# Second layer's feed-forward up: one piece of 512 columns, with shift times root in its sources

## The chip, the cores and the metric

The kernel runs on one core of one Trainium2 chip. The metric is device time in microseconds (us) of one launch; before the change the median of three runs is 2778.01 us. The core has five engines that run side by side and wait for one another by semaphores: TensorE (PE) for matmuls, VectorE (DVE), ScalarE (ACT), GpSimd (POOL) and SyncE (SP), which here only starts DMAs. PE takes its operands from SBUF and writes to PSUM, in banks of 512 float32 columns.

## The reference

Two layers of a first block, then a second block that the change does not touch. The part that matters is the feed-forward of a layer, for the main stream of 512 tokens with D = 1024 features (in layer 1 also for a context of 256 tokens; in layer 2 the context is no longer needed, `need_ctx` is false):

```python
def rmsnorm(t, g):
    return t * rsqrt(mean(t * t, axis=-1) + EPS) * g
def modulate(t, shift, scale):
    return t * (1 + scale) + shift
def conv_ffn(h, w_up, conv_w, conv_b, w_down):        # w_up: 1024 x 5632
    u = h @ w_up
    up = jnp.pad(u, ((0, 0), (1, 1), (0, 0)))
    u = up[:, :-2] * conv_w[0] + up[:, 1:-1] * conv_w[1] + up[:, 2:] * conv_w[2] + conv_b
    a, b = jnp.split(u, 2, axis=-1)
    return (jax.nn.silu(a) * b) @ w_down
h = h + mx[5] * conv_ffn(modulate(rmsnorm(h, norm2_g[l]), mx[3], mx[4]), w_up[l], ...)
```

## The kernel before

Features lie on the 128 partitions, tokens in the columns, so the residual h is 8 tiles (KT = 8) of 128 partitions x 512 tokens in layer 2. Products are computed to nearly float32 accuracy from rounded operands: a value is split into a high half (rounded, made by ACT) and a low half (the rest, made by DVE), and a product is three matmuls, high x low, high x high and low x high. Each matmul is preceded by one weight load of 128 x 128.

**The stage.** `ffn_up` is one stage: all engines meet at a barrier at its start and end. It has FT = 22 blocks i, each with two halves c (c = 0 goes through Silu, c = 1 is its factor), and for each half (i, c) PE goes through the 8 source tiles k with three products each. The halves' sums lie in two pairs of PSUM areas, by i modulo 2. The high parts of the weights have one room for each c, shared by all blocks: ACT (`high`, L2017) may write the one of (i + 1, c) only when (i, c) is done, and DVE (`low`, L2052) makes the low part after it. The weights come in strips by DMA, one for each block; those of block 0 are split in the stage before.

**The normalisation is deferred.** With g the gain (norm weight times 1 + scale) and s the shift, the product of w with (g x h x r + s) is r x (w, g x h) + (w, s), where r is one over the root of the mean square, a number for each token. So the sources of the matmuls are the tiles g x h, and two columns behind them hold s (for the two streams): 514 columns in layer 2, cut into 256 and 258. They are split by `Deferred.high` and `Deferred.low`, six of eight tiles (LOWS_AHEAD = 6) completely beside the output projection, the stage ahead of this one, through its hooks `add` (on ACT, when DVE has finished a unit of h) and `after` (on DVE). So block 0 can start at once. The squares, their sum, the mean (a matmul with ones, `mean`), Sqrt (`root`) and the reciprocal (`invert`) are made beside blocks 0 and 1.

**What follows a half.** DVE (`evict`): copies the two columns (w, s) out of PSUM to `bias` (L2057), and multiplies the product by r (L2059). ACT (`shift`, L2022) adds the bias. DVE (`convolve`, L2068 to L2070) waits for that and does the convolution over tokens. ACT does Silu (L2027), DVE the product of the halves (L2077). The order on DVE is: low weights of the next block's half, `evict`, `convolve` of the half before, and the product of the block before.

The output projection (`output_projection`, `project`) has 8 units of 512 columns, 8 tiles with three matmuls (L953) each; DVE's sum into h is L1919. After the feed-forward up comes the feed-forward down, again by `project`.

## Time and profile before

| | us |
|---|---|
| median of three runs | 2778.01 |
| the three runs | 2770.65, 2778.01, 2778.29 |
| the profiled execution | 2779.62 |
| its span, first to last instruction | 2777.8 |
| feed-forward up of layer 2, first matmul to last | 1460.1 to 1718.5 |

The profile is of one execution. Times in it count from the start of the span. A matmul's own duration holds the filling and draining of the array, and one starts before the last has ended; the distance between starts is what counts. PEclk is TensorE's granted clock as a share of 2.4 GHz. In a timeline row "xN" says how many instructions in a row it takes together, and the bracket how long the engine stood idle before it and who released it.

### The profile page before, as it was taken

Reading aid. Unit: us, or ns where it says so; the run is one execution under the profiler, and the core shown is the slowest. Engines: PE = TensorE matmul, PEld = TensorE weight load, DVE = VectorE, ACT = ScalarE, POOL = GpSimd, SP = SyncE. Lnnn points to the kernel's source line nnn. Section 1 sums busy time; section 2 is a strip of 40 time slices with the busy share of each in tenths; the row PEclk is TensorE's granted clock in tenths of the full one; section 3 lists DMA queues with packets and bytes.
Section 4 is the critical chain, followed back from the end, with each engine's and each line's share of the span. In section 5 each row is a group of like instructions: output and inputs, shape, how many; then the busy total and the mean of one; then the engine's idle time right before and its main releaser. Section 6 shows DMA issues by size and latency. Waiting matters only on the chain. (4 is left out here: it accounts for less than half of the span.)

```text
span 2777.8 us, 34833 instructions
## 1 busy us (share of the span) xinstructions
PE 2487.8 (90%) x14602; PEld 1933.5 (70%) x14602; DVE 1375.2 (50%) x2185; ACT 868.5 (31%) x1385; POOL 251.7 (9%) x183
## 2 busy tenths in 40 slices
PE   7997988999998998997889999998977889898976
PEld 5885657888887787995669998764733368573322
DVE  4324554566667214325647777347565645423213
ACT  3222433332324113223444334233424642311001
POOL 0002520000000000003500000000042020011112
PEclk9998989999999999997989999999988999988999
DMA  5114731111111112115612223320201013348997
GB/s 240 61 54 106 269 128 46 46 61 61 63 69 38 53 63 82 61 69 142 224 46 92 92 92 117 111 82 31 87 0 54 0 61 137 121 188 326 421 421 292
DMA packets 58555, 326.88 MB, mean 118 GB/s; under 512 B 8157, under 2 KB 14429, under 8 KB 26461
## 3 DMA queue, kind: packets, MB, share of 16 engines
q1 hardware_dynamic: 45358, 302.76, 29.4%
q0 software_dynamic: 5696, 12.59, 1.2%
q10 hardware_dynamic: 7344, 9.28, 1.0%
q8 instruction: 117, 1.92, 0.3%
q14 instruction: 40, 0.33, 0.0%
HBM read 317.26 MB, written 12.58 MB: 119 GB/s over the span
## 5 line engine op out<-in xcount | busy, mean ns | idle before, releaser
L953 PE MATMUL ps<-work_rounded,ring_rounded 128*128 128x512 f32 (+1 forms) x2016 | 537.0, 354 | 19.1 <-DVE work_rounded L397 10.6
L953 PE MATMUL ps<-xn_rounded,ring_rounded 128*128 128x512 f32 (+2 forms) x2304 | 541.8, 347 | 0.0
L2003 PE MATMUL ps<-xn_rounded,ring_rounded 128*128 128x258 f32 (+2 forms) x2816 | 535.1, 312 | 0.0
L2003 PEld LDWEIGHTS ps<-xn_rounded,ring_rounded 128*128 128x128 f32 x2816 | 414.6, 191 | 31.2
L953 PEld LDWEIGHTS ps<-xn_rounded,ring_rounded 128*128 128x128 f32 x2304 | 373.4, 191 | 57.6 <-issue 0.2
L953 PEld LDWEIGHTS ps<-work_rounded,ring_rounded 128*128 128x128 f32 x2016 | 336.5, 192 | 76.3 <-DVE work_rounded L397 11.8
L953 PE MATMUL ps<-big_rounded,ring_rounded 128*128 128x512 f32 (+1 forms) x1200 | 326.3, 364 | 45.0 <-DVE big_rounded L859 25.0
L859 DVE TENSOR_TENSOR ring_rounded<-ring,ring_rounded 128x2048 fp32r<-128x2048 f32 (+2 forms) x94 | 189.1, 2015 | 266.5 <-ACT ring_rounded L824 266.5
L2003 PE MATMUL ps<-work_rounded,ring_rounded 128*128 128x256 f32 (+1 forms) x1232 | 280.2, 309 | 9.0 <-PEq L784 4.8
L953 PEld LDWEIGHTS ps<-big_rounded,ring_rounded 128*128 128x128 f32 x1200 | 203.4, 196 | 84.8 <-DVE ring_rounded L859 21.4
L824 ACT ACTIVATE ring_rounded<-ring 128x2048 fp32r<-128x2048 f32 (+2 forms) x94 | 158.2, 1687 | 314.7 <-PE ps L953 298.3
L2003 PEld LDWEIGHTS ps<-work_rounded,ring_rounded 128*128 128x128 f32 x1232 | 191.9, 191 | 21.5 <-issue 10.6
L2052 DVE TENSOR_TENSOR ring_rounded<-ring,ring_rounded 128x1024 fp32r<-128x1024 f32 x84 | 103.0, 1226 | 171.4 <-ACT ring_rounded L2017 171.4
L2017 ACT ACTIVATE ring_rounded<-ring 128x1024 fp32r<-128x1024 f32 x84 | 89.0, 1060 | 205.8 <-PE ps L2003 205.8
L2022 ACT ACTIVATE work<-work,small 128x512 f32<-128x512 f32 (+1 forms) x132 | 81.5, 649 | 203.0 <-DVE work L2059 203.0
L1313 ACT ACTIVATE big<-big,small 128x512 f32<-128x512 f32 (+1 forms) x81 | 47.0, 624 | 254.0 <-DVE big L1309 154.0
L1303 DVE COPY small<-ps 128x2 f32<-128x2 f32 x46 | 7.3, 159 | 176.9 <-PE ps L953 176.6
L3320 PE MATMUL ps<-big,work 128*64 128x512 f32 x352 | 80.4, 604 | 15.1 <-DMA big<-in_experts 13.8
L1339 POOL MEMSET work<- 128x792 f32 x2 | 1.5, 758 | 1015.4 <-DMA work<-in_pool 1015.4
L2070 DVE SCALAR_TENSOR_TENSOR work<-work,vec 128x769 f32<-128x769 f32 (+1 forms) x88 | 78.0, 887 | 3.1
L2069 DVE SCALAR_TENSOR_TENSOR work<-work,vec 128x769 f32<-128x769 f32 (+1 forms) x88 | 78.0, 887 | 3.1
L3343 ACT ACTIVATE work<-ps,small 128x256 f32<-128x256 f32 x16 | 7.6, 476 | 221.3 <-PE ps L3320 221.3
(420 smaller groups left out, 3125.4 us busy)
## 6 DMA issues: line engine op xcount, KB each, us to landing
ring<-in_stream SPq DMA_DIRECT2D x141, 1024.0 KB, 4.8
big<-in_experts SPq DMA_DIRECT2D x44, 1024.0 KB, 26.0
ring<-in_stream SPq DMA_DIRECT2D x32, 704.0 KB, 4.0
ring<-in_experts SPq DMA_DIRECT2D x22, 1024.0 KB, 27.3
xn<-in_experts SPq DMA_DIRECT2D x15, 1024.0 KB, 28.4
work<-in_experts SPq DMA_DIRECT2D x15, 1024.0 KB, 28.7
big<-in_first_modulation SPq DMA_DIRECT2D x8, 1024.0 KB, 14.1
work<-in_bias ACTq DMA_DIRECT2D x24, 256.0 KB, 3.9
```

The lines of the kernel that those rows point to most:

```text
L824: return act.activation(self.rounded(high), value, ACT.Copy)
L859: return dve.tensor_tensor(self.rounded(value), value, self.rounded(high).bitcast(F32), ALU.subtract)
L953: mm = pe.matmul(out[:, a - u.first:b - u.first], lhs, rhs, start=j == 0 and n == 0 and not u.onto, stop=j == terms - 1 and n == len(passe ...
L1313: act.activation(px[:, m, a:z], px[:, m, a:z], ACT.Identity, bias=bias[:, m, s:s + 1])
L2003: mm = pe.matmul(out[:, a:b], ws[:, k, :], x[k][:, a - base:b - base], start=k == 0 and n == 0, stop=k == KT - 1 and n == 2)
L2017: act.activation(high_w[c], half(i, c)[0], ACT.Copy).then_inc(strip_high.up(), 1)
L2022: ins = act.activation(u[:, i % 2, c, o:o + b - a], u[:, i % 2, c, o:o + b - a], ACT.Identity, bias=bias[:, i % 2, c, s:s + 1])
L2052: dve.tensor_tensor(low_part, value, high_w[c].bitcast(F32), ALU.subtract).then_inc(strip_low.up(), 1)
L2069: settle(dve, dve.scalar_tensor_tensor(out=cc, in0=uu[:, 0:n], scalar=cw(0, t), in1=cc, op0=ALU.mult, op1=ALU.add), vstep)
L2070: dve.scalar_tensor_tensor(out=cc, in0=uu[:, 2:2 + n], scalar=cw(2, t), in1=cc, op0=ALU.mult, op1=ALU.add).then_inc(convolved.up(), 1)
L3320: mm = pe.matmul(b.bank(2)[r, :], self.rows_t[:, k, r], self.gu[s][:, k, :], start=k == 0, stop=k == KT - 1)
L3343: act.activation(self.silu_t, b.bank(2)[:, 0:256], ACT.Silu, scale=b.slot_scale[:, 0, n:n + 1]).then_inc(self.silued, 1)
```

## The change

For layer 2 alone (`need_ctx` false) a class `Rooted` takes the place of `Deferred`. Since g x h x r + s = r x (g x h + s x root), the sources become g x h + s x root, and the product need only be multiplied by r. The two extra columns, their copy and ACT's shift are gone, and a source is 512 columns, one matmul in place of two. In the output projection ACT now writes g x h and the square of each tile, and DVE adds the squares up; the stage begins with the mean and the root, then each tile is shifted by DVE, split by ACT and DVE, and used by both halves of block 0 in turn, tile by tile. Layer 1 computes as before.

The core of the diff ("..." marks what is left out):

```diff
+class Rooted(Deferred):
+    def square(self, act, k):
+        squared, added = self.b.sig("squared"), self.b.sig("squares_added")
+        act.activation(self.rooms[k][0], self.b.x[:, k, :], ACT.Identity, scale=self.gain(k))
+        if k >= 4:
+            act.wait_ge(added.sem, added.at(k - 3))
+        act.activation(self.squares[0] if k == 0 else self.squares[1 + (k - 1) % 3], self.b.x[:, k, :], ACT.Square).then_inc(squared.up(), 1)
+    def add_square(self, dve, k):
...
+    def mean(self, pe, area):
+        pe.matmul(area[:, 0:S], self.b.ones, self.squares[0], start=True, stop=True).then_inc(self.b.sig("summed").up(), 1)
...
+    def shifted(self, dve, k):
+        value = self.rooms[k][0]
+        return dve.scalar_tensor_tensor(out=value, in0=self.root_area, scalar=self.shift(k), in1=value, op0=ALU.mult, op1=ALU.add)
...
-        if next_sources:
+        if type(next_sources) is Rooted:
+            add, after = next_sources.square, next_sources.add_square
+        elif next_sources:
...
-        cuts = [(base, 512), (512, T + 2)]
+        cuts = [(0, 512), (512, T + 2)] if need_ctx else [(0, S)]
...
+                if not need_ctx:
+                    deferred.mean(pe, products[1][1])
+                    for k in range(KT):
+                        pe.wait_ge(tile_low.sem, tile_low.at(k + 1))
+                        for c in range(2):
+                            products_of(0, c, k)
+                    self.strips_freed(1)
...
+                else:
+                    deferred.root(act, products[1][1])
+                    for k in range(KT):
+                        act.wait_ge(tile_value.sem, tile_value.at(k + 1))
+                        deferred.high(act, k).then_inc(tile_high.up(), 1)
+                    high(1, 0)
...
-                    shift(i, c)
+                    if need_ctx:
+                        shift(i, c)
...
-                dve.tensor_copy(bias[:, i % 2, c, :], ps[:, T:T + 2])
+                    if need_ctx:
+                        dve.tensor_copy(bias[:, i % 2, c, :], ps[:, T:T + 2])
...
-                    dve.wait_ge(shifted.sem, shifted.at(2 * i + c + 1))
+                    ready = shifted if need_ctx else evicted
+                    dve.wait_ge(ready.sem, ready.at(2 * i + c + 1))
...
+                else:
+                    dve.wait_ge(self.sig("rooted").sem, self.sig("rooted").at(1))
+                    deferred.shifted(dve, 0).then_inc(tile_value.up(), 1)
+                    for k in range(KT):
+                        if k + 1 < KT:
+                            deferred.shifted(dve, k + 1).then_inc(tile_value.up(), 1)
+                        dve.wait_ge(tile_high.sem, tile_high.at(k + 1))
+                        deferred.low(dve, k).then_inc(tile_low.up(), 1)
                 low(1, 0)
                 deferred.invert(dve)
```

What stands in a row on TensorE at the stage's start, before (L953 ends the output projection, L2003 are the products):

```order
L953 MATMUL ps<-work_rounded,ring_rounded 128x512 x2
L784 UNCONDITIONAL_BRANCH
L1986 UNCONDITIONAL_BRANCH [waits barrier_Pool_Activation_PE_DVE_SP_release]
L2003 MATMUL ps<-work_rounded,ring_rounded 128x256
L2003 MATMUL ps<-work_rounded,ring_rounded 128x258
L2003 MATMUL ps<-xn_rounded,ring_rounded 128x256
L2003 MATMUL ps<-xn_rounded,ring_rounded 128x258
```

and after (L477 is the mean, L2045 are the products):

```order
L1000 MATMUL ps<-work_rounded,ring_rounded 128x512 x2
L831 UNCONDITIONAL_BRANCH
L2039 UNCONDITIONAL_BRANCH [waits barrier_Pool_Activation_PE_DVE_SP_release]
L477 MATMUL ps<-work,base 128x512
L2045 MATMUL ps<-work_rounded,ring_rounded 128x512 [waits tile_low]
L2045 MATMUL ps<-xn_rounded,ring_rounded 128x512 x2
L2045 MATMUL ps<-work_rounded,ring_rounded 128x512
L2045 MATMUL ps<-xn_rounded,ring_rounded 128x512 x2
L2045 MATMUL ps<-work_rounded,ring_rounded 128x512 [waits tile_low]
```

The mean has moved from the front of block 1 to the front of block 0, every sixth matmul of block 0 waits for a tile's low half, and a pair has become one.

On VectorE, from the last sum of the output projection to the first scaling, before (L394 and L397 are the last two low halves, L412 adds squares, L448 is the reciprocal):

```order
L1919 SCALAR_TENSOR_TENSOR h<-ps,mods,h 128x512 [waits product_done]
L784 UNCONDITIONAL_BRANCH
L2047 UNCONDITIONAL_BRANCH [waits barrier_Pool_Activation_PE_DVE_SP_release]
L394 SCALAR_TENSOR_TENSOR work_rounded<-h,gains,xn_rounded 128x512
L397 TENSOR_TENSOR work_rounded<-mods,xn_rounded 128x2
L394 SCALAR_TENSOR_TENSOR work_rounded<-h,gains,xn_rounded 128x512
L397 TENSOR_TENSOR work_rounded<-mods,xn_rounded 128x2
L412 TENSOR_TENSOR work<-work 128x512 [waits squared]
L412 TENSOR_TENSOR work<-work 128x512 [waits squared,squares_added] x6
L2052 TENSOR_TENSOR ring_rounded<-ring,ring_rounded 128x8x128 [waits strip_high,squares_added]
L448 RECIPROCAL big<-big 128x512 [waits rooted]
```

and after, the start (L474 adds squares, L486 shifts a tile, L906 is its low half):

```order
L474 TENSOR_TENSOR work<-work 128x512 [waits squared]
L831 UNCONDITIONAL_BRANCH [waits squares_added]
L2119 UNCONDITIONAL_BRANCH [waits barrier_Pool_Activation_PE_DVE_SP_release]
L486 SCALAR_TENSOR_TENSOR work<-big,mods,work 128x512 [waits rooted]
L486 SCALAR_TENSOR_TENSOR work<-big,mods,work 128x512
L906 TENSOR_TENSOR work_rounded<-work,xn_rounded 128x512 [waits tile_high]
L486 SCALAR_TENSOR_TENSOR work<-big,mods,work 128x512
```

and, eight tiles on, its end (L2124 are low halves of weights, L495 the reciprocal, L2132 the scaling):

```order
L906 TENSOR_TENSOR work_rounded<-work,xn_rounded 128x512 [waits tile_high] x2
L2124 TENSOR_TENSOR ring_rounded<-ring,ring_rounded 128x8x128 [waits strip_high]
L495 RECIPROCAL big<-big 128x512
L2132 TENSOR_TENSOR work<-ps,big 128x512 [waits product_done,zeroed,vector_step]
L2124 TENSOR_TENSOR ring_rounded<-ring,ring_rounded 128x8x128 [waits strip_high]
```

The first DVE instructions of the stage now wait for the root, and the last adding of squares has moved ahead of the barrier; the reciprocal stays between the low weights of (1, 0) and those of (1, 1).

## Rows read from the trace of the kernel before

**Rows 1.** The page, first part: each engine's busy time and share.

```profile
PE 2487.8 (90%) x14602; PEld 1933.5 (70%) x14602; DVE 1375.2 (50%) x2185; ACT 868.5 (31%) x1385; POOL 251.7 (9%) x183
```

**Rows 2.** TensorE's waits in the stage, with releaser: total, times, longest us.

```profile
PE ps L2003 <- DVE ring_rounded L2052: 2.2, 1, 2.2
PE ps L2003 <- PEq L784: 2.0, 1, 2.0
```

**Rows 3.** Table by stretches: output projection, then the stage, both at full clock.

```profile
core 0: us, PE busy (x) PEld busy (x) DVE busy (x) ACT busy (x) POOL busy (x), PEclk, DMA share, GB/s
1417.27:1457.70 40.43, 40.43 (x176) 32.83 (x175) 16.77 (x24) 11.23 (x18) 0.00 (x0) 1.00 0.22 78
1482.13:1718.54 236.41, 236.40 (x1968) 236.20 (x1968) 180.71 (x280) 90.97 (x114) 0.00 (x0) 1.00 0.24 87
```

**Rows 4.** The same table for the first layer's feed-forward up.

```profile
540.00:850.00 310.00, 310.00 (x1759) 271.94 (x1758) 196.59 (x294) 94.09 (x129) 0.00 (x0) 1.00 0.18 64
```

**Rows 5.** Timeline where the stage starts: start us, length us, engine, line, operation.

```profile
1458.14 0.75 DVE L1919 SCALAR_TENSOR_TENSOR h<-ps,mods,h 128x512 f32<-128x512 f32 x1 [3.81 <-PE ps L953]
1458.93 0.72 ACT L387 ACTIVATE xn_rounded<-h,gains 128x512 fp32r<-128x512 f32 x1 [4.48 <-DVE h L1919]
1459.55 0.19 ACT L389 ACTIVATE xn_rounded<-mods 128x2 fp32r<-128x2 f32 x1
...
1460.08 5.03 ACT L405 ACTIVATE work<-h 128x512 f32<-128x512 f32 x8 [0.33 <-PEq L784]
```

**Rows 6.** Timeline: a mean's matmul at full clock; 768 columns at half.

```profile
1473.19 1.02 PE L437 MATMUL ps<-work,base 128*128 128x512 f32 x2
...
1109.81 2.93 PE L437 MATMUL ps<-work,base 128*128 128x512 f32 x4 [2.77 <-DVE work L412]
```

**Rows 7.** Timeline of ScalarE: Sqrt, and a table load with what follows it.

```profile
1474.25 0.60 ACT L443 ACTIVATE big<-ps 128x512 f32<-128x512 f32 x1 [4.19 <-PE ps L437]
...
1487.27 1.28 ACT L2027 ACT_TABLE_LOAD   x1
1488.56 0.63 ACT L2027 ACTIVATE work<-work 128x512 f32<-128x512 f32 x1
```

**Rows 8.** VectorE: splits in the output projection; a group, its count, total, mean ns.

```profile
1410.00 4.91 DVE L859 TENSOR_TENSOR big_rounded<-big,work_rounded 128x512 fp32r<-128x512 f32 x8 [1.02 <-ACT work_rounded L824]
...
1428.30 2.29 DVE L859 TENSOR_TENSOR ring_rounded<-ring,ring_rounded 128x2048 fp32r<-128x2048 f32 x1 [1.96 <-ACT ring_rounded L824]
...
L412 DVE TENSOR_TENSOR work<-work 128x512 f32<-128x512 f32 x7 | 4.8, 691 | 0.2
```

**Rows 9.** Table by stretches where stages start; PEclk 0.50 is 1.2 GHz.

```profile
1457.70:1461.15 3.45, 1.45 (x11) 1.08 (x10) 1.80 (x4) 1.89 (x5) 1.09 (x1) 0.99 0.55 188
1461.15:1464.56 3.41, 3.41 (x19) 3.41 (x18) 3.27 (x7) 3.09 (x7) 1.59 (x1) 0.51 0.30 123
1411.34:1416.46 5.12, 5.12 (x14) 3.97 (x12) 4.59 (x7) 4.07 (x6) 0.00 (x0) 0.50 0.00 0
1724.58:1730.90 6.32, 6.32 (x15) 4.97 (x16) 5.69 (x10) 6.32 (x13) 0.00 (x0) 0.51 0.82 247
```

**Rows 10.** ScalarE's weight splits (a group); VectorE's and TensorE's rows before half (1, 1).

```profile
L2017 ACT ACTIVATE ring_rounded<-ring 128x1024 fp32r<-128x1024 f32 x42 | 44.5, 1059 | 63.6 <-PE ps L2003 63.6
...
1474.88 3.35 DVE L448 RECIPROCAL big<-big 128x512 f32<-128x512 f32 x1 [4.80 <-ACT big L443]
...
1480.76 1.23 DVE L2052 TENSOR_TENSOR ring_rounded<-ring,ring_rounded 128x1024 fp32r<-128x1024 f32 x1 [1.74 <-ACT ring_rounded L2017]
...
1482.13 0.47 PE L2003 MATMUL ps<-work_rounded,ring_rounded 128*128 128x256 f32 x2 [2.17 <-DVE ring_rounded L2052]
```

**Rows 11.** Timeline where the stage's matmuls have ended.

```profile
1718.57 0.16 DVE L2057 COPY small<-ps 128x2 f32<-128x2 f32 x1 [0.63 <-PE ps L2003]
...
1719.37 0.72 ACT L2022 ACTIVATE work<-work,small 128x512 f32<-128x512 f32 x1 [3.23 <-DVE work L2059]
...
1720.61 0.75 DVE L2070 SCALAR_TENSOR_TENSOR work<-work,vec 128x512 f32<-128x512 f32 x1
```

More of the change, by code:

```diff
@@ L448, in invert, with __init__, root, high @@
         settle(dve, dve.reciprocal(self.rstd, self.rstd), vstep)
+class Rooted(Deferred):
+    def __init__(self, b, l, rooms, squares, root, rstd):
+        self.b, self.rooms, self.root_area, self.rstd = b, rooms, root, rstd
+        self.first, self.width = CTX, S
+        self.squares = tiles_in(S, squares)[0:4]
+        self.gain = lambda k: b.gains[:, l, 0, 1, k:k + 1]
+        self.shift = lambda k: b.mods[:, l, 0, 3 * KT + k:3 * KT + k + 1]
+    def square(self, act, k):
[5 more added lines that the diff above has]
+    def add_square(self, dve, k):
+        squared, added = self.b.sig("squared"), self.b.sig("squares_added")
+        if k >= 1:
+            dve.wait_ge(squared.sem, squared.at(k + 1))
+            settle(dve, dve.tensor_tensor(self.squares[0], self.squares[0], self.squares[1 + (k - 1) % 3], ALU.add), added)
+    def mean(self, pe, area):
+        pe.matmul(area[:, 0:S], self.b.ones, self.squares[0], start=True, stop=True).then_inc(self.b.sig("summed").up(), 1)
+    def root(self, act, area):
+        summed, rooted = self.b.sig("summed"), self.b.sig("rooted")
+        act.wait_ge(summed.sem, summed.at(1))
+        act.activation(self.root_area, area[:, 0:S], ACT.Sqrt, scale=1.0 / D, bias=EPS).then_inc(rooted.up(), 1)
+    def shifted(self, dve, k):
+        value = self.rooms[k][0]
+        return dve.scalar_tensor_tensor(out=value, in0=self.root_area, scalar=self.shift(k), in1=value, op0=ALU.mult, op1=ALU.add)
+    def high(self, act, k):
+        return self.b.split_high(act, *self.rooms[k])
+    def low(self, dve, k):
+        return self.b.split_low(dve, *self.rooms[k])
+    def invert(self, dve):
+        settle(dve, dve.reciprocal(self.rstd, self.root_area), self.b.sig("vector_step"))
 class FilterFeatures:
@@ L1987, in _, with products_of @@
             def _(pe):
-                for i, c in halves_of:
-                    if (i, c) == (1, 0):
+                def products_of(i, c, k):
+                    out, high, low = products[i % 2][c], high_w[c], half(i, c)[1]
+                    for n, (ws, x) in enumerate(((high, low_x), (high, high_x), (low, high_x))):
+                        for a, b in cuts:
+                            mm = pe.matmul(out[:, a:b], ws[:, k, :], x[k][:, a:b], start=k == 0 and n == 0, stop=k == KT - 1 and n == 2)
+                    if k == KT - 1:
+                        mm.then_inc(done.up(), 1)
+                if not need_ctx:
+                    deferred.mean(pe, products[1][1])
[4 more added lines that the diff above has]
+                    self.strips_freed(1)
+                for i, c in halves_of[0 if need_ctx else 2:]:
+                    if (i, c) == (1, 0) and need_ctx:
                         deferred.mean(pe, products[1][1])
@@ L1996, in _ @@
                         pe.wait_ge(strip_low.sem, strip_low.at(2 * (i - 1) + c + 1))
-                    out, high, low = products[i % 2][c], high_w[c], half(i, c)[1]
                     for k in range(KT):
@@ L2000, in _ @@
                             pe.wait_ge(tile_low.sem, tile_low.at(k - LOWS_AHEAD + 1))
-                        for n, (ws, x) in enumerate(((high, low_x), (high, high_x), (low, high_x))):
-                            for a, b in cuts:
-                                mm = pe.matmul(out[:, a:b], ws[:, k, :], x[k][:, a - base:b - base], start=k == 0 and n == 0, stop=k == KT - 1 and n == 2)
-                    mm.then_inc(done.up(), 1)
+                        products_of(i, c, k)
                     if c == 1:
@@ L2027, in silu @@
                     act.activation(cv[:, i % 2, 0, 0:n], cv[:, i % 2, 0, 0:n], ACT.Silu).then_inc(silued.up(), 1)
[L2029 to L2032 removed]
+                if need_ctx:
+                    for k in range(KT):
+                        deferred.square(act, k)
+                    high(1, 0)
+                    deferred.root(act, products[1][1])
+                else:
+                    deferred.root(act, products[1][1])
+                    for k in range(KT):
+                        act.wait_ge(tile_value.sem, tile_value.at(k + 1))
+                        deferred.high(act, k).then_inc(tile_high.up(), 1)
+                    high(1, 0)
                 for i, c in halves_of:
```

20 lines of the change are left out of this document (11 added, 9 removed).

## The prediction, made before the changed kernel was run

> **What bounds the kernel now.** The page's first part comes first: TensorE (PE) is busy for 90% of the span and no other engine for more than 50% [rows 1]. The share alone decides nothing, so the next view is the table of waits for the stage that the change touches, the second layer's feed-forward up (from 1460.1 to 1724.2 us). PE waits there 2.0 us for the start of the stage and 2.2 us once for VectorE's (DVE's) low half of a weight strip, and not otherwise [rows 2]. The third view is the table by stretches: from 1482.13 to 1718.54 us PE, at full clock, has 1968 matmuls in 236.41 us and no gap; DVE has 180.7 us of work beside it and ScalarE (ACT) 91.0 us [rows 3]. So the stage lasts as long as its matmuls, and anything taken from DVE or ACT in its middle is worth nothing. What counts is the time of a matmul, and what PE waits for at the stage's two ends.
>
> **1. Two matmuls of 256 and 258 columns become one of 512.** 1968 matmuls in 236.41 us are 120.1 ns each, 240.3 ns for the pair [rows 3]. For the new one the nearest row is the output projection just ahead: same clock, same kind of operands, same order of weight halves, 512 columns in one piece: 175 matmuls start between 1417.27 and 1457.70 us, 231.0 ns each [rows 3] (the row counts one more, which began before). A second bound comes from the first layer's feed-forward up, which runs 512 and 258 columns by turns: 1759 matmuls in 310.0 us, 352.5 ns a pair [rows 4]; less 120.1 for the piece of 258 that leaves 232.4 ns. The saving is 7.9 to 9.3 ns a pair; I take 9.3, since that row is wholly of the new shape. One matmul carries one weight load: these are busy for all of the stretch of pairs (236.2 of 236.41 us) and for 32.8 of 40.43 us in the other [rows 3], which is a reason for the gain. The stage has 22 blocks of 2 halves of 24 pairs. From the second half of block 1 to the end are 41 halves, 984 pairs: 9.1 us less (7.8 by the other row).
> The Trainium skill (TensorE: Matmul & The Clock Gate, section Back-to-back issue gap) gives a warm matmul N / 2.4 + 2.5 ns, so that one matmul fewer would save only that constant, less the two columns: about 3.3 ns a pair, an estimate by that page. The rows above disagree with it (120.1 ns, where it has 109 to 110, and 231.0, where it has 216); with it the 984 pairs would give 3.3 us.
>
> **2. The start of the stage.** Before, PE starts at once on sources that were split beside the output projection; the root of the mean square is needed only for scaling the result. Now the sources hold the shift times the root, so nothing of block 0 can start before the root. Followed in time of the profile before:
> DVE's last sum in the output projection starts when its last matmul is done, at 1458.1, and ends at 1458.9 [rows 5]. ACT then did a scaled copy, 0.62 us to its next instruction [rows 5]; a Square is new there (eight in a row take 5.03 us, some 0.62 each [rows 5]): done at 1460.2. DVE's last adding of squares, new here too, takes 0.69 us (group L412 [rows 8]) and ends at 1460.9. From the last ACT instruction (1459.55 + 0.19) to the first of the next stage are 0.34 us [rows 5], so the stage starts at 1461.25, 1.2 us later than now.
> The mean is a matmul of 512 unrounded columns. Warm it takes 1.02 us; at half clock 512 and 256 columns took 2.93 us together, so 2.0 us for the 512 [rows 6]. Here the clock fell at 1461.15, after a stretch in which PE was busy for 1.45 of 3.45 us [rows 9]; with PE idle from 1458.1 to 1461.25 it has more reason to. I take 2.0: 1463.25. The table load for Sqrt (1.28 us) lies beside it. Sqrt 0.60 [rows 7]: 1463.9. DVE's first shifted tile 0.75: 1464.65. ACT's high half 0.63, as for the Silu of the same size [rows 7]: 1465.3. DVE has the second shifted tile in its queue ahead of the first low half, and that holds it to 1465.35; the low half 0.69: 1466.05, PE starts at 1466.1. (The tile's form is that of DVE's sum at 1458.14, 0.75 us [rows 5]; the low half's is that of the eight splits in 4.91 us, 0.61 each in a row [rows 8] and 0.69 alone. So a row saves 0.08, and the tile is 0.67 in one.)
> The Trainium skill (ScalarE: Activation LUTs, section What ACT_TABLE_LOAD costs) adds a drain of 1.38 us to every load. The trace shows none: the load at 1487.27 takes 1.28 us and the activation behind it starts at 1488.56 [rows 7]. With it Sqrt would start at 1463.9 rather than 1463.3, and the sum would be 0.6 us worse.
> Block 0 now goes tile by tile, 6 matmuls for each. DVE needs 0.67 + 0.61 = 1.3 us for a tile, PE 6 x 0.231 = 1.39 warm and 6 x 0.427 = 2.56 at half clock (12 weight loads, one for each matmul, in 5.12 us [rows 9]), so PE sets the pace, though narrowly. The clock: with PE at work from their start, three stages show half clock for 3.4 us (1461.15 to 1464.56), at least 5.1 (1411.34 to 1416.46) and 6.3 (1724.58 to 1730.9) [rows 9]. I take 5.1; each us of it costs 0.46 us (1 - 231/427). Block 0: 48 x 0.231 + 5.1 x 0.46 = 13.4 us, to 1479.5.
>
> **3. The wait in front of block 1.** High halves of the weights have one room for each half block, so ACT can split those of (1, 0) only when (0, 0) is done. Going tile by tile, (0, 0) now ends only three matmuls, 0.7 us, before the block's end: 1478.9 with the drain. ACT 1.06 us, DVE 1.23 (L2017 and L2052 [rows 10]): PE gets (1, 0) at 1481.4, a wait of 1.9 us, that took no time before. (1, 0) lasts 24 x 0.231 = 5.54 us: 1486.95. Behind it, what was late before (the wait of 2.17 us, from the reciprocal of 3.35 us that had to come first [rows 10]) is now just hidden: DVE does the reciprocal from 1481.35 to 1484.7, the scaling to 1485.4, the low half of (1, 1) to 1486.6, some 0.4 us before PE asks for it. If that cover is gone, each us more costs one.
> So (1, 1) starts at 1486.95 in place of 1482.13: 4.8 us worse.
>
> **4. Taken away at nothing.** 44 shifts on ACT (0.72 us) and 44 copies of two columns on DVE (0.16 us, half of it overlapped) [rows 11] in the stage's middle: hidden by PE, which never waits there. At the end the copy at 1718.57 stands on the path and saves 0.1 us; the last shift (1719.37 to 1720.1) lies beside the convolution of the other half, which runs until 1721.36 [rows 11], and saves nothing.
> **5. Added beside the output projection.** A Square for each tile, in place of a copy of two columns: ACT's split of the next weights comes 0.4 us later, and DVE's, which waits for it and ends at 1430.6 [rows 8], too. PE asks for that strip when it comes to unit 4; with 5.54 us for a unit and the last of 8 done at 1458.1 that is at 1435.9. With 5 us of cover this costs nothing.
>
> **The sum:** + 4.8 - 9.1 - 0.1 = - 4.4 us. Against the profiled execution (2779.6 us, of which 2777.8 are the span) that is 2775.2; the median of the runs shown is 1.6 us lower, so 2773.6.
>
> **Rivals.**
> A, slower: *the clock stays at half through block 0.* PE works in groups of 6 with DVE just ahead of it, and its waits could keep the clock down. All 48 matmuls at 427 ns are 20.5 us, 7.1 more: + 2.7, 2780.7. It decides from 14.7 us of half clock (5.1 + 4.4 / 0.46). Against it: at half clock PE needs 2.56 us a tile and DVE 1.3, so PE has no gap by which it could stay down, and none of the three starts shows over 6.3 us. Chance 4 in 100.
> B, slower too: *a matmul's time goes by its columns alone* in this stage. Then one of 512 would cost 240.3 x 512 / 514 = 239.3 ns and save 1.0 ns, 8.3 less than I count, in 1008 pairs: + 4.0, 2782.0. It decides from a saving of 4.9 ns a pair. Both rows of the new shape speak against it [rows 3, 4]. Chance 3 in 100. By the constant of the Trainium skill (TensorE: Matmul & The Clock Gate, Back-to-back issue gap) it would be 6.0 ns x 1008 and 2779.6.
> C: *the clock falls again* in the wait of 1.9 us in front of block 1, as it did after the 2.0 us at 1458 but not after the 2.17 us at 1480 (the stretch from 1482.13 has the full clock throughout [rows 3]). Half clock for 3.4 us: + 1.6, 2775.2. Chance 20.
> D: *a kinder start*: the mean warm (- 1.0) and half clock for only 3.4 us (- 0.8): - 6.2, 2771.8. Chance 15.
> E: *faster by over 8.3 us.* The stage alone would have to give 4 us more than the forecast and 2 more than D; only stretches of half clock elsewhere could: the runs of before lie between 2770.65 and 2779.62. Chance 10. As much the other way (a tile chain that binds, DVE's slack of 0.4 us gone, a run on the high side) 4.
> The forecast itself, within 1.5 us, has 44.
>
> **How the numbers follow.** 0.3% is 8.3 us, about what a measurement of this kernel can tell from no change. Faster by more: E, 10, and a little of D, 12 in all. Slower by more: 4, out of the last case and the far ends of A and B. Within: 84. The range from 2768.0 to 2779.8 takes in C and D, the 1.3 us by which the price of a matmul is open, and the spread of runs; A, B and most of E are left out.
>
> **What would show it.** The stage's matmuls should start 231 ns apart, with weight loads busy for four fifths; the mean should start at about 1461.25, the first of block 0 at 1466.1, with PE idle for 3 us between; block 0 should take 13 to 14 us; one wait of 1.9 us on DVE stands before block 1 and none after; the last matmul starts near 1714. A pitch of 235 or more, a first block over 16 us, or waits of PE for DVE at the tiles would make the prediction wrong.

## The result, and the profile of the changed kernel

| | median us | runs | lowest to highest |
|---|---|---|---|
| before | 2776.40 | 20 | 2770.65 to 2780.28 |
| after | 2783.78 | 20 | 2773.73 to 2791.40 |

The ratio is 1.0024, 95% interval 1.0016 to 1.0031: 7 us slower where 3 to 4 us faster were forecast, and 4 us above the end of the range. The profiled execution of after took 2783.89 us, with a span of 2782.1. One run of all that follow, an execution of a_pad_busy of 3304.76 us, was in a slower state and is left out of that kernel's range.

The 20 times of after fall in two groups: five from 2773.73 to 2775.10, and fifteen from 2780.94 to 2791.40. Five times the forecast was met, fifteen times something of about 10 us came on top. That suggests that the working of the stage was not the main error; it does not show it, since the profile is of one execution, of the upper group.

The page's first part, after (answering to [rows 1]):

```profile
PE 2489.1 (89%) x13546; PEld 1878.8 (68%) x13546; DVE 1376.4 (49%) x2141; ACT 841.3 (30%) x1341; POOL 251.6 (9%) x183
```

TensorE has 1056 matmuls fewer than before and is busy for 1.3 us more. Matmuls have become fewer and somewhere others have become slower.

**The changed stage went nearly as forecast.** First the waits of TensorE in it, after (answering to [rows 2]): line waited with, releaser, total, times, longest.

```profile
PE ps L477 <- PEq L831: 3.5, 1, 3.5
PE ps L2045 <- DVE work_rounded L906: 3.0, 1, 3.0
PE ps L2045 <- DVE ring_rounded L2124: 1.8, 1, 1.8
```

Then the timeline of its start, TensorE's, ScalarE's and VectorE's rows (start us, length us, engine, line):

```profile
1454.49 0.69 DVE L474 TENSOR_TENSOR work<-work 128x512 f32<-128x512 f32 x1 [1.31 <-ACT work L468]
1455.74 1.28 ACT L482 ACT_TABLE_LOAD   x1 [1.28 <-PEq L831]
...
1455.79 1.10 PE L477 MATMUL ps<-work,base 128*128 128x512 f32 x2 [3.46 <-PEq L831]
1457.04 0.60 ACT L482 ACTIVATE big<-ps 128x512 f32<-128x512 f32 x1
1457.67 1.41 DVE L486 SCALAR_TENSOR_TENSOR work<-big,mods,work 128x512 f32<-128x512 f32 x2 [2.48 <-ACT big L482]
...
1459.86 0.79 PE L2045 MATMUL ps<-work_rounded,ring_rounded 128*128 128x512 f32 x1 [2.98 <-DVE work_rounded L906]
```

And the table by stretches (columns as in [rows 3]), from the start of the output projection's last matmul to half (1, 1), and from there to the start of the stage's last matmul:

```profile
1451.94:1457.30 5.36, 1.48 (x4) 0.30 (x2) 1.44 (x2) 2.79 (x4) 1.55 (x1) 1.00 0.55 196
1457.30:1464.10 6.80, 4.24 (x10) 3.37 (x11) 6.40 (x10) 3.49 (x6) 1.12 (x1) 0.50 0.01 2
1464.10:1480.71 16.61, 14.84 (x64) 11.61 (x63) 10.95 (x13) 3.90 (x5) 0.00 (x0) 1.00 0.18 63
...
1480.71:1710.07 229.36, 229.36 (x984) 184.80 (x983) 177.50 (x238) 60.83 (x72) 0.00 (x0) 1.00 0.25 89
```

The first three rows add up to 28.8 us from the projection's last matmul to (1, 1). Before it was 24.4 (1457.71 to 1482.13), and the forecast, 1457.71 to 1486.95, was 29.2. The reading to learn here is how such a start is put together: a barrier, a mean, a root, two tiles, one split, each with its row, and the first product where the sum says. The last row is the stage's long part: 984 matmuls that start within 229.36 us, 233.3 ns from one start to the next (983 distances). The pairs of before, read in the same way to the start of the last, took 236.13 us:

```profile
1482.13:1718.26 236.13, 236.12 (x1968) 236.13 (x1968) 180.71 (x280) 90.97 (x114) 0.00 (x0) 1.00 0.24 87
```

In after the weight loads are busy for 184.8 of 229.36 us, four fifths as foreseen. So from the projection's end to the stage's end the change is worth - 6.8 + 4.4 = - 2.4 us: half of the forecast's 4.4, with the right sign.

**The loss is 130 us further on, in code that the change does not touch.** Behind the feed-forward down, which is the same in both, comes the stage that makes the filters of the hyena part. It begins with 16 matmuls of 65 rows and 512 columns in plain float32, each of them two records (the operand column says 65*128). The timeline of TensorE there, kernel before:

```profile
1851.26 0.87 PE L953 MATMUL ps<-big_rounded,ring_rounded 128*128 128x512 f32 x3
1853.30 13.97 PE L2192 MATMUL ps<-work,big 65*128 65x512 f32 x32 [1.18 <-PEq L784]
```

and kernel after:

```profile
1842.84 0.87 PE L1000 MATMUL ps<-big_rounded,ring_rounded 128*128 128x512 f32 x3
1844.88 26.17 PE L2275 MATMUL ps<-work,big 65*128 65x512 f32 x32 [1.18 <-PEq L831]
1870.85 9.74 PE L2287 MATMUL ps<-big,work 128*128 128x512 f32 x19
```

The same idle time of 1.18 us ahead, the same 32 records, but 26.17 us in place of 13.97. The table by stretches has the reason in its column PEclk. Before:

```profile
1845.00:1853.00 8.00, 7.12 (x31) 5.37 (x29) 3.04 (x2) 1.34 (x1) 0.00 (x0) 1.00 0.23 82
1853.00:1868.00 15.00, 13.97 (x32) 6.01 (x33) 11.49 (x20) 8.05 (x12) 0.00 (x0) 1.00 0.20 70
1868.00:1883.00 15.00, 13.97 (x32) 5.99 (x32) 13.79 (x23) 8.91 (x15) 0.00 (x0) 1.00 0.00 1
```

After:

```profile
1838.00:1844.80 6.80, 5.71 (x25) 4.23 (x23) 2.99 (x2) 0.00 (x0) 0.00 (x0) 1.00 0.20 66
1844.80:1846.40 1.60, 1.52 (x4) 0.83 (x5) 0.17 (x1) 1.55 (x2) 0.00 (x0) 0.99 0.68 225
1846.40:1855.00 8.60, 8.60 (x12) 3.41 (x11) 4.07 (x6) 4.82 (x8) 0.00 (x0) 0.50 0.17 73
1855.00:1871.00 16.00, 16.00 (x20) 6.22 (x19) 11.35 (x18) 7.86 (x12) 0.00 (x0) 0.50 0.00 1
1871.00:1875.00 4.00, 4.00 (x8) 1.73 (x7) 3.72 (x7) 1.33 (x2) 0.00 (x0) 0.66 0.00 0
1875.00:1907.00 32.00, 28.75 (x67) 11.09 (x65) 19.42 (x32) 4.34 (x8) 0.00 (x0) 1.00 0.00 1
```

In after the granted clock fell to 0.50 (1.2 GHz) at 1846.4 us, 1.5 us into the filters, and stayed there although TensorE has no gap until 1871. It came back only when the matmuls of 128 rows had begun (1870.85; the stretch 1871 to 1875 has 0.66). The whole stage took 63.35 us in place of 51.91, from VectorE's last instruction ahead of it to its last in it: 11.4 us more. Behind it every stage edge of after lies 3.0 us behind that of before, unchanged to the end of the layer. So the two traces differ by this, by the same edges: 5.3 us that after had gained before the output projection began, in stages that are the same in both; 2.8 us gained in the projection and the changed stage; 0.3 in the feed-forward down; and 11.4 us lost in the filters.

The theory that the experiments had to try: the filters' stage begins with an idle time in either kernel; whether the clock falls there depends on when it begins, against moments that the kernel does not set; the changed kernel moved the stage and so met a bad moment more often; and matmuls of 65 rows, once at half clock, don't bring it back. Rivals: the loss belongs to something the change itself does (memory that it holds, a transfer), or it is chance.

### The profile page after: what moved, and what is told of

Same layout as the page of the kernel before. It is cut to its first block and busy times, and to the rows that moved or that the text cites. A ratio compares the mean times of both kernels' runs of the same rounds, so it can differ in the third digit from the quotient of the medians.

```text
span 2782.1 us, 32633 instructions
## 1 busy us (share of the span) xinstructions
PE 2489.1 (89%) x13546; PEld 1878.8 (68%) x13546; DVE 1376.4 (49%) x2141; ACT 841.3 (30%) x1341; POOL 251.6 (9%) x183
## 5 line engine op out<-in xcount | busy, mean ns | idle before, releaser
L2045 PE MATMUL ps<-xn_rounded,ring_rounded 128*128 128x512 f32 x2112 | 530.3, 359 | 0.0
L1000 PEld LDWEIGHTS ps<-xn_rounded,ring_rounded 128*128 128x128 f32 x2304 | 373.5, 191 | 57.5 <-issue 0.2
L2045 PEld LDWEIGHTS ps<-xn_rounded,ring_rounded 128*128 128x128 f32 x2112 | 352.9, 190 | 63.3
L1000 PEld LDWEIGHTS ps<-work_rounded,ring_rounded 128*128 128x128 f32 x2016 | 335.8, 192 | 76.3 <-DVE work_rounded L397 11.7
L906 DVE TENSOR_TENSOR ring_rounded<-ring,ring_rounded 128x2048 fp32r<-128x2048 f32 (+2 forms) x94 | 189.1, 2015 | 263.9 <-ACT ring_rounded L871 263.9
L2045 PE MATMUL ps<-work_rounded,ring_rounded 128*128 128x512 f32 x880 | 277.7, 364 | 9.5 <-DVE ring_rounded L2124 3.8
L2124 DVE TENSOR_TENSOR ring_rounded<-ring,ring_rounded 128x1024 fp32r<-128x1024 f32 x84 | 102.9, 1226 | 170.4 <-ACT ring_rounded L2081 170.4
L2045 PEld LDWEIGHTS ps<-work_rounded,ring_rounded 128*128 128x128 f32 x880 | 149.3, 191 | 38.3 <-issue 5.4
L2086 ACT ACTIVATE work<-work,small 128x512 f32<-128x512 f32 x88 | 49.5, 611 | 112.2 <-DVE work L2132 112.2
L2132 DVE TENSOR_TENSOR work<-ps,big 128x512 f32<-128x512 f32 (+1 forms) x132 | 74.7, 594 | 1.2 <-PE ps L2045 1.1
```

The lines of the kernel that those rows point to most:

```text
L906: return dve.tensor_tensor(self.rounded(value), value, self.rounded(high).bitcast(F32), ALU.subtract)
L1000: mm = pe.matmul(out[:, a - u.first:b - u.first], lhs, rhs, start=j == 0 and n == 0 and not u.onto, stop=j == terms - 1 and n == len(passe ...
L2045: mm = pe.matmul(out[:, a:b], ws[:, k, :], x[k][:, a:b], start=k == 0 and n == 0, stop=k == KT - 1 and n == 2)
L2086: ins = act.activation(u[:, i % 2, c, o:o + b - a], u[:, i % 2, c, o:o + b - a], ACT.Identity, bias=bias[:, i % 2, c, s:s + 1])
L2124: dve.tensor_tensor(low_part, value, high_w[c].bitcast(F32), ALU.subtract).then_inc(strip_low.up(), 1)
L2132: ins = dve.tensor_tensor(u[:, i % 2, c, o:o + b - a], ps[:, at:at + b - a], deferred.rstd[:, a:b], ALU.mult)
```

## The experiments

There were four comparisons, each on one chip with its own runs of before (medians 2776.91, 2776.84, 2777.31 and 2776.05 us). "a" is the changed kernel and "b" the kernel before, with an edit. Added matmuls write a bank that nobody reads.

| kernel | comparison | median us | lowest to highest | ratio to before, 95% |
|---|---|---|---|---|
| b_delay9 | 1 | 2790.64 | 2778.34 to 2794.10 | 1.0037 (1.0022 to 1.0052) |
| a_delay5 | 1 | 2777.18 | 2774.07 to 2789.36 | 1.0001 (0.9989 to 1.0013) |
| b_pad | 1 | 2777.72 | 2771.70 to 2788.90 | 1.0003 (0.9991 to 1.0015) |
| a_pad | 1 | 2775.12 | 2770.56 to 2778.44 | 0.9995 (0.9984 to 1.0006) |
| a_pad_two | 2 | 2769.89 | 2766.12 to 2780.36 | 0.9977 (0.9966 to 0.9987) |
| b_pad_delay9 | 2 | 2780.80 | 2776.92 to 2785.32 | 1.0020 (1.0011 to 1.0029) |
| a_pad_early | 2 | 2771.14 | 2767.96 to 2775.22 | 0.9982 (0.9973 to 0.9991) |
| a_pad_busy | 2 | 2769.43 | 2765.12 to 2774.77 | 0.9977 (0.9967 to 0.9986) |
| a_pad_again | 3 | 2777.51 | 2772.99 to 2780.71 | 0.9996 (0.9987 to 1.0005) |
| a_pad_two_again | 3 | 2776.11 | 2772.10 to 2780.15 | 0.9994 (0.9985 to 1.0003) |
| a_pad_delay5 | 3 | 2777.72 | 2776.29 to 2782.39 | 1.0001 (0.9992 to 1.0011) |
| a_pad_two_delay5 | 3 | 2777.51 | 2767.42 to 2786.05 | 0.9995 (0.9982 to 1.0007) |
| after_again | 4 | 2782.34 | 2772.52 to 2793.26 | 1.0021 (1.0009 to 1.0032) |
| a_two | 4 | 2775.01 | 2766.13 to 2780.97 | 0.9996 (0.9984 to 1.0007) |
| a_pad_busy_again | 4 | 2771.48 | 2765.99 to 2774.92 | 0.9983 (0.9974 to 0.9992) |
| a_pad_third | 4 | 2776.01 | 2769.55 to 2780.18 | 1.0000 (0.9991 to 1.0009) |

### The kernel before, shifted: b_delay9

Nine small matmuls in the feed-forward down of layer 2, ahead of the filters; nothing of the change.

```diff
+        if i == 6:
+            for _ in range(9):
+                pe.matmul(b.bank(5, 128), b.ones, b.ones, start=True, stop=True)
         if i == 4:
```

> The kernel before, with nine extra matmuls of ones by ones (128 unrounded columns each, into an unused bank) in unit 6 of the second layer's feed-forward down; their result is read by nobody. They take about 2.2 us of TensorE. Theory (the clock at the next stage is a matter of when that stage begins): before ends its feed-forward down at 1852.1 and the next stage, whose matmuls of 65 rows run at L2192, keeps full clock; 2.2 us later its beginning stands where that of the changed kernel stood, the clock falls and these matmuls stay at half clock, so + 2.2 + about 11, some 2789 against 2776. Rival (the loss comes from something the change does to data, memory or queues): + 2.2 alone, 2778 to 2779, and the L2192 matmuls stay at 14 us.

Measured: 13.7 us above before. In the trace the feed-forward down is 1.9 us longer (130.6 in place of 128.7 us, by VectorE's last instructions), and the filters' group (line, engine, shape, count, busy, mean ns, idle before) reads:

```profile
L2195 PE MATMUL ps<-work,big 65*128 65x512 f32 x32 | 26.2, 1015 | 1.2 <-PEq L787 1.2
```

So the loss comes in a kernel that has none of the change, only from a shift. The rival that the change's own memory or transfers do it falls.

### The changed kernel, shifted: a_delay5

The same edit on the changed kernel, with five.

> The changed kernel with five such extra matmuls (about 1.2 us of TensorE) in the same place. Theory of the clock: the next stage begins 1.2 us later against the moments at which the clock is set anew, where before's began, so its first matmuls stay at full clock more often: most executions near 2775 to 2776 instead of 2784, although 1.2 us of work are added. Rival (data, memory or queues): 2785.

```profile
L2278 PE MATMUL ps<-work,big 65*128 65x512 f32 x32 | 14.0, 594 | 1.2 <-PEq L834 1.2
```

Work added, and 6.6 us less than after (from another comparison). The rival "work on the path alone" would have given 2785.

### The rows padded: b_pad and a_pad

The filters' operands get 128 rows, the 63 added ones zero, so that the same products are made by full matmuls.

```diff
-                    pe.matmul(self.bank(u % 8), h[0:65, t * P:(t + 1) * P], filt[0:65, column(o, d)], ...
+                    pe.matmul(self.bank(u % 8), h[:, t * P:(t + 1) * P], filt[:, column(o, d)], ...
```

> The kernel before, with the filter stage's 16 matmuls (L2192) given 128 rows in place of 65: zeros in rows 65 to 127 of both operands, the table 128 rows long. Same results. If matmuls of 65 rows are what can't bring the clock back, padding costs nothing where the clock does not fall: 2776, within 3 us of before, since in the profile of before it does not fall there.

> The changed kernel with the same padding. Theory: a full matmul brings the clock back after one step, so a fall at the stage's beginning costs 2 to 4 us and not 12; the stage at L2275 takes 14 to 18 us, the median falls from 2784 to 2775 to 2777, and the two groups of times (2774 to 2775 and 2781 to 2791) come together. Then the change itself is worth - 1 to - 3 us against the padded kernel before. Rival (the fall is due to a longer idle time or to the operands' data, not to the rows): the padded kernel stays near 2784.

In a_pad the group takes what the 65-row group takes at full clock:

```profile
L2276 PE MATMUL ps<-work,big 128*128 128x512 f32 x32 | 14.0, 594 | 1.2 <-PEq L832 1.2
```

The padding costs nothing in these records and takes the upper group of times away: no run of a_pad is above 2778.44, where fifteen of twenty of after were above 2780.9 (nor is any of its 22 later runs above 2780.71). On before it changes nothing that can be measured, since the times of before seldom lie in that group. Single high runs have other causes as well: b_pad has one of 2788.90, and no trace shows what it was. The two side by side estimate what the change is worth without the accident: 2775.12 against 2777.72, - 2.6 us, near the - 2.4 of the two traces; but the intervals of the two ratios overlap, so the runs by themselves do not show a gain. In all there are 12 traces of padded kernels here, and none has a fall of the clock in the filters; of six unpadded ones three have it (after, b_delay9, after_again), 1.5, 1.5 and 1.8 us behind the first filter matmul.

The theory's moments can be read from the traces too. In each of the 18 all steps of the granted clock, down and up, fit one even row of moments to within 0.005 us; only where the row lies against the kernel differs. The first moment behind the first filter matmul comes after:

| | us | clock falls there |
|---|---|---|
| 65 rows: after, b_delay9, after_again | 1.50, 1.49, 1.84 | yes |
| 65 rows: a_two, before, a_delay5 | 1.39, 0.32, 0.28 | no |
| 128 rows: a_pad_third, a_pad, b_pad_delay9 | 1.49, 1.61, 1.70 | no |

The other nine padded traces have 0.1 to 1.4 or 2.3 to 3.0. So the same stage behind the same idle time falls or does not fall by where it stands against the moments. And three padded traces stand where the unpadded ones fell: the padding did not make a fall short, as was expected, it kept it away. That 128-row matmuls bring the clock back is seen only behind the filters of the three unpadded traces that fell.

### A shift with the rows padded: b_pad_delay9

b_pad and b_delay9 together.

> The kernel before with padded filter matmuls and the nine extra matmuls (1.9 us measured). Without padding they made it 13.7 us slower. If the loss is the matmuls of 65 rows that stay at half clock, it is now 1.9 us plus at most 3 for a fall that is made good: 2780 to 2782 against 2777.7. If the moment of the stage's beginning costs in some other way: 2788 and more.

Measured 4 us above before, where b_delay9 was 13.7 above: of the shift's price some 10 us were the filters', 1.9 the matmuls' own, and some 2 us are not accounted for; that the other stages behind lie against the clock's moments in another way too is a guess.

### The change without the merging: a_pad_two, twice, and the delays

The sources and the order of the changed kernel, but two pieces of 256 columns in two banks.

```diff
-        cuts = [(0, 512), (512, T + 2)] if need_ctx else [(0, S)]
+        cuts, apart = ([(0, 512), (512, T + 2)], 0) if need_ctx else ([(0, 256), (256, S)], 256)
...
-                            mm = pe.matmul(out[:, a:b], ws[:, k, :], x[k][:, a:b], ...
+                            mm = pe.matmul(out[:, a + apart:b + apart], ws[:, k, :], x[k][:, a:b], ...
```

> The changed kernel with padded filter matmuls, its products cut again into two pieces of 256 columns (in two banks): all of the change but the merging. If the merging is what is gained, starts are 120 ns apart (240 for a pair, against 233.3 for one of 512), the 41 last halves take 236 us and not 229.4, and the kernel is 6.8 us slower than the padded changed one: 2782 against 2775. Rival (the 256 + 258 of before were slow for the two columns or the banks): 2775 to 2778.

A miss: 2769.89 us, below the merged kernel (a_pad, in comparison 1) by 5. Its stage in the table by stretches, (1, 1) to the start of the last matmul:

```profile
1484.59:1716.26 231.67, 231.67 (x1970) 231.67 (x1968) 177.30 (x238) 60.90 (x72) 0.00 (x0) 1.00 0.25 89
```

231.67 us: between the pairs of before (236.1) and the merged ones (229.4). So of the 6.8 us that the new shape brings, 4.5 come with the sources' losing two columns (the two pieces begin at the same places in the banks, 256 and 512, as the pairs of before), and 2.3 with one matmul in place of two, which lies in one bank. The median below the merged kernel's had no reason in this trace, whose own run (2780.36) was the slowest of the eight. Hence both kernels again on one chip, each also with the five added matmuls:

> The changed kernel with the 65-row matmuls of the filters padded to 128 rows, once more, so that it stands on the same chip as the three runs beside it. If the 5 us between it (2775.1) and the version with two pieces of 256 columns (2769.9) belong to the kernels, it gives 2774 to 2776 again. If they belong to the chip of that comparison, it comes out within 2 us of the two-piece version.

> The same with two pieces of 256 columns in two banks, once more. Its one trace has 231.67 us for the 41 last halves where the merged piece has 229.36, so by the stage alone it is 2.3 us slower than the merged one: 2777 to 2778. If its runs stay at 2768 to 2771, the other stages give the rest, by where they lie against the moments at which the clock is set, and another trace should show shorter half-clock stretches outside of this stage.

> a_pad_again with five small matmuls added in the feed-forward down of layer 2 (1.2 us of work, as in a_delay5). If all that counts is the work on the path, 1.2 us over a_pad_again. If the moments at which the clock is set matter to the stages behind, the difference is another, by up to 5 us either way.

> a_pad_two_again with the same five matmuls. If two pieces are faster as such (by 5 us), it stays some 5 us below a_pad_delay5. If the two-piece version only lay well against the moments at which the clock is set, the gap to a_pad_delay5 changes by more than 2 us, up to the other sign (2.3 us above it).

2777.51 and 2776.11; with the added work 2777.72 and 2777.51. All four intervals overlap: the 5 us were not the kernels' in general. The shift by 1.2 us of work cost 0.2 and 1.4 us. But with the delay the two-piece kernel spreads wider (2767.4 to 2786.1, against 2776.3 to 2782.4 for the merged one; without it both spread by 8 us), and the next kernel shows a possible reason.

### The changed kernel again, and with two pieces: after_again, a_two

> The changed kernel once more, on another chip. By the theory (65-row matmuls stay at half clock for some 11 us longer when the stage begins at a bad moment) the times fall in two groups again, most of them 5 us and more above the padded version beside it: median 2782 to 2785. By the rival (the loss was that chip's, or chance) it stands within 2 us of the padded version.

> The changed kernel with two pieces of 256 columns in two banks instead of one of 512, no padding. The stage takes 2.3 us longer than the merged one. If what happens to the filters is set by when their stage begins, this shift of 2.3 us later does what the 1.2 us of added matmuls did: most runs have the filters at full clock, median 2776 to 2779, below after_again in spite of more work. By the rival (work on the path alone) it is 2.3 us above after_again, 2785 to 2787.

Another chip, the same picture: after_again 2782.34 with nine of twelve runs above 2780, and the padded version beside it (a_pad_third) 2776.01. Its trace has the fall too:

```profile
1841.00:1850.00 9.00, 8.10 (x35) 6.16 (x33) 3.04 (x2) 1.92 (x1) 0.00 (x0) 1.00 0.23 73
1850.00:1852.00 2.00, 1.72 (x4) 0.87 (x5) 0.17 (x1) 1.75 (x2) 0.00 (x0) 1.00 0.75 270
1852.00:1876.00 24.00, 24.00 (x30) 9.50 (x29) 15.42 (x24) 12.46 (x19) 0.00 (x0) 0.50 0.05 22
```

a_two has more matmuls and no padding, and is 7.3 us faster than after_again; its filters ran at full clock:

```profile
L2275 PE MATMUL ps<-work,big 65*128 65x512 f32 x32 | 14.0, 594 | 1.2 <-PEq L831 1.2
```

Not all of that is the filters. In this execution its two-piece stage went at another pace than in the three traces of padded two-piece kernels, with the same instructions there:

```profile
1482.65:1705.58 222.93, 222.93 (x1970) 222.93 (x1968) 177.44 (x239) 60.85 (x72) 0.00 (x0) 1.00 0.26 92
```

222.93 us, 113.3 ns a matmul in place of 117.8, from the first half to the last, 8.7 us less. It was seen in one of four traces of that shape, in none of the ten of the merged one (229.4 each time), and in none of the four of before's pairs (236.1 each). It may be what made the runs of comparison 2 so fast; since only one run of each kernel is profiled, that stays open. So does what sets the pace.

### Better starts: a_pad_early, a_pad_busy and a_pad_busy_again

a_pad_early takes the last four tiles of block 0 for its first half and then for its second, so that (0, 0) ends earlier and the weights of (1, 0) can be split under the rest.

```diff
-                        for c in range(2):
+                        for c in range(2 if k < 4 else 1):
                             products_of(0, c, k)
+                    for k in range(4, KT):
+                        products_of(0, 1, k)
```

> The changed kernel, padded, with the last four tiles of block 0 done first for half 0 and then for half 1. Half (0, 0) then ends 12 matmuls (2.8 us) before the block's end and not 3 (0.7), so that the weights of (1, 0) are split beside (0, 1). The wait of 1.8 us in front of (1, 0) goes: 2773.3 against 2775.1. If something else is late there (the strip, the low tiles): no gain.

a_pad_busy also gives TensorE twelve small matmuls behind the output projection and twelve behind the mean, so that it is not idle while the root is made.

```diff
+                    for _ in range(12):
+                        pe.matmul(self.bank(5, 128), self.ones, self.ones, start=True, stop=True)
```

> The same with TensorE kept at work while it would wait: 12 small matmuls of ones by ones (0.2 us each, into an unused bank) at the end of the output projection and 12 behind the mean. If half clock at the start of block 0 costs what was counted (about 2.3 us, and 1.0 for the mean), this gives 2 to 3.3 us more: 2770.5 against 2773.3. If the small matmuls do not hold the clock, or hold up what they stand before: 2773 to 2775.

The waits of TensorE in the stage, a_pad_early and then a_pad_busy:

```profile
PE ps L477 <- PEq L832: 3.5, 1, 3.5
PE ps L2046 <- DVE work_rounded L907: 3.0, 1, 3.0
```

```profile
PE ps L477 <- PEq L832: 0.8, 1, 0.8
PE ps L2049 <- DVE work_rounded L907: 0.6, 2, 0.3
```

The wait of 1.8 us in front of (1, 0) is gone in both, and in the second the fillers stand where TensorE was idle; timeline:

```profile
1454.76 2.84 PE L1010 MATMUL ps<-base 128*128 128x128 f32 x24
1458.38 1.10 PE L477 MATMUL ps<-work,base 128*128 128x512 f32 x2 [0.78 <-PEq L832]
1459.31 2.84 PE L2056 MATMUL ps<-base 128*128 128x128 f32 x24
1462.46 0.50 PE L2049 MATMUL ps<-work_rounded,ring_rounded 128*128 128x512 f32 x1 [0.30 <-DVE work_rounded L907]
```

In a_pad_busy the clock does not fall at the stage's start, and the stage (between VectorE's last instructions) takes 261.8 us in a_pad (260.9 in a_pad_third), 258.9 in a_pad_early and 257.6 in a_pad_busy. Against before the medians are 5.7 and 7.4 us lower; a_pad_early was not run again. Since the comparison before had shown a version 5 us off, the second was put beside a_pad once more:

> Padding, the last tiles of block 0 taken for its first half before its second, and small matmuls that keep TensorE busy at the stage's start. The traces gave 4.2 us less for the stretch from the projection's end to the stage's end than the padded version alone. If that belongs to the kernel, it stands 3 to 5 us below a_pad_third here too, 2771 to 2774; if it was the chip, within 2 us of it.

> The changed kernel with padded filters, as the neighbour of the three others on this chip. 2774 to 2778, as twice before.

2771.48 beside 2776.01: 4.5 us less than the padded kernel on the same chip (from the projection's last matmul to the stage's last, the two traces of this comparison differ by 3.2 us, 254.9 and 258.1), 4.6 us less than before, ratio 0.9983 (0.9974 to 0.9992). In both comparisons this version is faster than before.

## Why the prediction was wrong

- **The step that failed is the frame of the sum.** It priced the stage that the change touches and took all work behind it as unchanged but for its start. The filters' stage was 11.4 us longer in the profiled run, and by the grouping of the times probably in three runs of four of after (15 of 20, and 9 of 12 in after_again; one trace of each shows it). The prediction had the material: rival C priced a fall of the clock where TensorE waits 1.9 us, but only next to the change, and for a length read from stretches with 128-row matmuls (3.4 us, + 1.6). A fall was on the list, but not there and not of that size. "Only stretches of half clock elsewhere could", said of rival E's gain, was true of a loss as well, and it had 4 chances in 100.
- **Section 1, the price of a matmul.** 231.0 ns was taken, 233.3 came: the gain of 984 pairs was 6.8 us and not 9.1. The layer-1 row, which was the other end (232.4 ns, 7.8 us), was nearer, though not far enough. The output projection that gave 231.0 has two paces itself, from the same instructions: by the starts of its last 170 matmuls it is 231.1 ns in seven of the 18 traces (before and a_pad among them) and 233.3 in the other eleven (after, a_pad_early, a_pad_busy, a_pad_third). The same stretch in after and in a_pad:

```profile
1413.00:1451.70 38.70, 38.70 (x167) 31.20 (x166) 16.09 (x17) 14.23 (x18) 0.00 (x0) 1.00 0.23 82
1413.00:1451.70 38.70, 38.70 (x170) 31.38 (x168) 16.10 (x17) 14.22 (x18) 0.00 (x0) 1.00 0.23 82
```

Before's trace happened to be of the quicker kind. So one execution's row of that shape is good to 1% only, which is 2.3 us in the sum. And most of the gain was put on the merging, while a_pad_two shows that two pieces of 256 keep 4.5 of the 6.8 us. The Trainium skill (TensorE: Matmul & The Clock Gate, Back-to-back issue gap) had 215.8 ns for 512 columns and 109.2 for 256 by its formula (an estimate; the section gives the formula for matmuls by themselves, not for a stream with weight loads); measured were 233.3, and 117.8 or 113.3: no run here comes as low.
- **Section 2, the start.** Right in the sum: mean to first product 4.07 us in after (forecast 4.85, with a mean at half clock; it ran at full, 1.10 us as in D, while in a_pad it ran at half and took 2.05); waits of 3.5 and 3.0 us. The clock was at half for 6.8 us, but 2.6 of them lay ahead of the first product, so block 0 had 4.2 us of half clock where 5.1 were counted. Together 28.8 us to (1, 1) in place of 29.2. No drain behind the table load: from its end (1457.02) to Sqrt (1457.04) there is nothing.
- **Section 3, the wait in front of block 1.** Right: 1.8 us (1.9), and no wait at (1, 1). a_pad_early shows that it was the room for the high weights: (0, 0) earlier, wait gone.
- **Sections 4 and 5.** Right: TensorE waits nowhere in the middle, and the squares beside the output projection show up in no wait.
- **Rivals A and B** fell: half clock in block 0 for 4.2 us and no more, and 6.8 ns less a pair where B had 1.0.
- With the filters padded the change stands 0 to 1.4 us below before by the ratios of three comparisons (0.9995, 0.9996 and 1.0000, none clear of 1), and 2.6 us below it where before is padded too: the forecast of 4.4 us less is off by 2 us and more there, of which 2.3 are the price of the matmul.
- **The level.** The forecast of 2773.6 started from the median of three runs, 2778.01; that of twenty is 2776.40. With it the same sum gives 2772.0 us (2776.4 - 4.4). So that the five lower runs of after (2773.73 to 2775.10) stand close to 2773.6 is in part luck.

## What to carry to other kernels

A change that shifts the work behind it is priced only when the stages behind it have been looked through for idle times, where TensorE's clock may fall, and for what would bring it back. In these traces matmuls that use only part of the rows were the ones to fear: padding them to 128 rows cost nothing and took away a loss of 11 us that most runs of the changed kernel seem to have had. Times that fall in two groups, or two versions that differ by more than their work, are the sign to look for this before the change is judged.

## What the runs showed of the hardware

- Matmuls of 65 rows, back to back with no gap, stayed at 1.2 GHz for 24.5 us after a fall (1846.4 to 1870.9) and the clock came back only behind the start of 128-row ones (1870.85); padded, the same 32 records never were at half clock in 12 traces. The same 1.18 us of idle time led to a fall in three of six traces without padding, and in none of the three padded ones that stood at the same place against the clock's moments (1.49 to 1.70 us). The Trainium skill (TensorE: Matmul & The Clock Gate, What's actually happening) says that the clock is set by a free-running window and that the same kernel therefore shows different numbers of slow matmuls from run to run; these traces agree (where the moments lie against the kernel differs from trace to trace, 0.28 to 1.84 us behind the first filter matmul in the unpadded ones). It puts the penalty of the slow start under 1% of a span; here one fall cost 0.4%, and still more than the change that was measured.
- The same instructions have more than one pace at full clock, kept through a whole stage: matmuls of 512 columns in the output projection 231.1 or 233.3 ns, those of 256 columns in the changed stage 117.8 or 113.3 (231.67 and 222.93 us), with weight loads busy all the time in both of the latter. No run shows what sets the pace.
- A version's ratio to before can move between chips by about the width of its interval: a_pad_two 0.9977 (0.9966 to 0.9987) and then 0.9994 (0.9985 to 1.0003).
